# Six up units of every chunk in seven block products, gate and up units in another order, weight sums on semaphores of their own

## The reference, cut to what matters

```python
h = rms_norm(x, norm_ffn[layer])                       # 256 x 2048
x = x + (silu(h @ w_gate) * (h @ w_up)) @ w_down       # 2048 x 5632, 2048 x 5632, 5632 x 2048
```

## Time and profile before

| what | us |
|---|---|
| median of 3 runs | 1379.51 |
| lowest and highest of them | 1379.26, 1391.07 |
| the profiled execution, its own time | 1378.64 |
| its span, first to last instruction | 1376.9 |
| PE busy in the span | 1362.5 (99%) |
| DVE busy | 922.5 (67%) |
| ACT busy | 702.5 (51%) |

### The profile page before, as it was taken

The page is one execution under the profiler, slowest core; times in us unless marked ns, Lnnn a source line. Parts: engine busy times, 40 slices in busy tenths (PEclk is TensorE's granted clock), DMA queues, the critical chain, the costliest instruction groups (busy, mean ns, idle before and its releaser), DMA issues.

```text
span 1376.9 us, 26434 instructions
## 1 busy us (share of the span) xinstructions
PE 1362.5 (99%) x11280; PEld 1325.5 (96%) x11280; DVE 922.5 (67%) x1192; ACT 702.5 (51%) x913; POOL 44.9 (3%) x70
## 2 busy tenths in 40 slices
PE   8999999999999999999999999999999999999997
PEld 7888999999999999999999999999999999999997
DVE  5554557667655657666787888875446778887554
ACT  6343356656545655465645554544334455545444
POOL 3000010000000110000000000000000000000111
PEclk9999999999999999999999999999999999999999
DMA  7776655444565666546556655565555565666653
GB/s 241 246 231 219 186 171 156 140 152 146 154 192 168 194 203 218 184 168 201 165 182 194 217 181 181 182 214 208 191 198 184 184 214 169 193 196 231 210 198 123
DMA packets 135264, 261.08 MB, mean 190 GB/s; under 512 B 8448, under 2 KB 25408, under 8 KB 134768
## 3 DMA queue, kind: packets, MB, share of 16 engines
q1 hardware_dynamic: 132912, 251.13, 57.0%
q0 software_dynamic: 1792, 7.57, 1.6%
q10 hardware_dynamic: 448, 0.76, 0.2%
HBM read 257.33 MB, written 2.10 MB: 188 GB/s over the span
## 4 chain that ended last, share of the span: by engine, by line
PE 88%; DVE 7%; ACT 2%; DMA 2%; issue 1%; ACTq 0%; DVEq 0%
PE bank L646 24%; PE bank L647 23%; PE bank L648 23%; PE bank L885 4%; PE bank L887 4%; PE bank L888 4%; DVE weight_lo_ring L1322 2%; PE bank L634 2%; DVE weight_sums_lo L1342 1%; ACT weight_hi_ring L1071 1%; DMA raw_ring<-in_w_up 1%; DVE weight_sums L1331 1%; PE bank L784 1%; DVE act_rows L1382 1%; PE bank L695 1%
## 5 line engine op out<-in xcount | busy, mean ns | idle before, releaser
L1322 DVE TENSOR_TENSOR weight_lo_ring<-raw_ring,weight_hi_ring 128x1024 fp32r<-128x1024 f32 (+2 forms) x479 | 579.9, 1221 | 319.2 <-ACT weight_hi_ring L1071 263.9
L1071 ACT ACTIVATE weight_hi_ring<-raw_ring 128x1024 fp32r<-128x1024 f32 (+2 forms) x431 | 446.2, 1047 | 343.4 <-PE bank L648 271.0
L646 PE MATMUL bank<-weight_hi_ring,hT_hi 128*128 128x256 f32 (+2 forms) x1276 | 380.9, 298 | 0.0
L648 PE MATMUL bank<-weight_hi_ring,hT_lo 128*128 128x256 f32 (+2 forms) x1276 | 375.5, 294 | 0.0
L647 PE MATMUL bank<-weight_lo_ring,hT_hi 128*128 128x256 f32 (+2 forms) x1276 | 375.5, 294 | 0.0
L646 PEld LDWEIGHTS bank<-weight_hi_ring,hT_hi 128*128 128x128 f32 x1276 | 239.8, 188 | 10.0 <-issue 3.4
L647 PEld LDWEIGHTS bank<-weight_lo_ring,hT_hi 128*128 128x128 f32 x1276 | 239.9, 188 | 6.1
L648 PEld LDWEIGHTS bank<-weight_hi_ring,hT_lo 128*128 128x128 f32 x1276 | 239.6, 188 | 6.3
L646 PE MATMUL bank<-weight_hi_ring,h2T_hi 128*128 128x256 f32 x704 | 196.5, 279 | 3.2 <-DVE weight_lo_ring L1322 3.1
L648 PE MATMUL bank<-weight_hi_ring,h2T_lo 128*128 128x256 f32 x704 | 195.3, 277 | 0.0
L647 PE MATMUL bank<-weight_lo_ring,h2T_hi 128*128 128x256 f32 x704 | 195.3, 277 | 0.0
(11 more groups left out here) (253 smaller groups left out, 1897.0 us busy)
## 6 DMA issues: line engine op xcount, KB each, us to landing
raw_ring<-in_w_in SPq DMA_DIRECT2D x96, 512.0 KB, 3.4
raw_ring<-in_w_gate SPq DMA_DIRECT2D x88, 512.0 KB, 4.3
raw_ring<-in_w_up SPq DMA_DIRECT2D x88, 512.0 KB, 4.2
raw_ring<-in_w_down SPq DMA_DIRECT2D x88, 512.0 KB, 3.9
raw_ring<-in_w_in SPq DMA_DIRECT2D x55, 480.0 KB, 4.2
raw_ring<-in_w_out SPq DMA_DIRECT2D x32, 512.0 KB, 4.0
raw_ring<-in_w_br_c SPq DMA_DIRECT2D x16, 256.0 KB, 3.9
raw_ring<-in_w_br_a SPq DMA_DIRECT2D x16, 256.0 KB, 6.8
```

The source lines that it names most:

```text
L646: pe.matmul(dst, x_hi, w_hi, start=opening, stop=False, skip_group_check=True)
L648: m = pe.matmul(dst, x_lo, w_hi, start=False, stop=last and k == UK - 1, skip_group_check=True)
L1071: act.activation(whi[:, s, :, 0:width(u)], raw[:, s, :, 0:width(u)], ACT.Copy)\
L1322: dve.tensor_tensor(lo, w, hi.bitcast(F32), ALU.subtract).then_inc(lo_ready, 1)
```

## The change

`SEVEN` takes unit 7 too, so 66 instead of 55 up units are done in seven products. Unit 7 is the last of its chunk, so the last product of each bank may now stand in a unit of seven (`stop`). The order of units in the middle of a half becomes u4 of the chunk before, g0, g1, g2, its u5, its u6, its u7, g3, g4, u0, g5, g6, u1, g7, u2, u3. ACT writes a unit's own hi first and its weight sums' hi after it; DVE writes the unit's own lo, then the sums' lo; the sums have two semaphores of their own, and PE waits for the second in the middle of the unit, after four of the seven products. `lo_of_act` on DVE comes three units later than before, except in the last chunk of a half.

```diff
-SEVEN = (0, 1, 2, 4, 5)
+SEVEN = (0, 1, 2, 4, 5, 7)
...
-            plan += g[0:6] if i == a else [g[0], last[4], g[1], last[5], g[2], last[6], last[7], g[3], g[4], g[5]]
-            plan += [up[0], g[6], up[1], g[7], up[2], up[3]]
+            plan += g[0:5] if i == a else [last[4], g[0], g[1], g[2], last[5], last[6], last[7], g[3], g[4]]
+            plan += [up[0], g[5], g[6], up[1], g[7], up[2], up[3]]
...
+ACT_LO_AT = {v if i + 1 in (b for _, b in HALVES) else v + LAG: i for v, i in ACT_T_AT.items()}
...
                 into(i, 6, 0, block(0, 0), quarters(u, 0, 0), True)
-                into(i, 3, 0, block(1, 0), quarters(u, 1, 0), False)
-                into(i, 2, 0, total(3), quarters(u, 1, 1), False)
+                into(i, 3, 0, block(1, 0), quarters(u, 1, 0), stop)
+                into(i, 2, 0, total(3), quarters(u, 1, 1), stop)
                 into(i, 6, 1, total(1), quarters(u, 0, 1), True)
+                pe.wait_ge(ext_ready, N_SEVEN[u] + 1)
                 into(i, 7, 0, total(0), extra(0), True)
                 into(i, 7, 1, total(2), extra(1), True)
-                return into(i, 2, 1, block(1, 1), extra(2), False)
+                return into(i, 2, 1, block(1, 1), extra(2), stop)
...
                 if is_seven(u):
-                    n = N_SEVEN[u]
-                    act.wait_ge(w_summed, n + 1)
-                    if n >= 2:
-                        act.wait_ge(unit_used, SEVENS[n - 2] + 1)
-                    act.activation(ext_hi[:, n % 2, :, :], t_sum[:, :, :], ACT.Copy)
+                    act.wait_ge(w_summed, N_SEVEN[u] + 1)
                 else:
                     act.wait_ge(raw_ready[s], landed(u))
                 act.activation(whi[:, s, :, 0:width(u)], raw[:, s, :, 0:width(u)], ACT.Copy)\
                    .then_inc(hi_ready, 2 if u == 1 else 1)
+                if is_seven(u):
+                    n = N_SEVEN[u]
+                    if n >= 2:
+                        act.wait_ge(unit_used, SEVENS[n - 2] + 1)
+                    act.activation(ext_hi[:, n % 2, :, :], t_sum[:, :, :], ACT.Copy).then_inc(ext_hi_ready, 1)
...
                 if n >= 1:
-                    dve.wait_ge(lo_ready, SEVENS[n - 1] + 1)
+                    dve.wait_ge(ext_ready, n)
...
+                split_unit(u % RING, u + 1, width(u))
                 if is_seven(u):
-                    e = N_SEVEN[u] % 2
-                    dve.wait_ge(hi_ready, u + 1)
-                    dve.tensor_tensor(ext_lo[:, e, :, :], t_sum[:, :, :], ext_hi[:, e, :, :].bitcast(F32), ALU.subtract)
-                split_unit(u % RING, u + 1, width(u))
+                    n = N_SEVEN[u]
+                    dve.wait_ge(ext_hi_ready, n + 1)
+                    dve.tensor_tensor(ext_lo[:, n % 2, :, :], t_sum[:, :, :], ext_hi[:, n % 2, :, :].bitcast(F32),
+                                      ALU.subtract).then_inc(ext_ready, 1)
...
-                if v in ACT_T_AT:
-                    lo_of_act(ACT_T_AT[v])
+                if v in ACT_LO_AT:
+                    lo_of_act(ACT_LO_AT[v])
```

More of the change, by code:

```diff
@@ L419, in build_layer @@
         w_summed = sem("weights_summed")
+        ext_hi_ready = sem("weight_sums_hi_ready")
+        ext_ready = sem("weight_sums_ready")
         silu_ready = sem("silu_ready")
```

## The result

The changed kernel took 1363.82 us (median of 4 executions, 1363.79 to 1364.32); the kernel before 1380.35 (median of 4, 1379.26 to 1391.07: the three shown above and one more, 1381.19). The ratio is 0.9864, 95% interval [0.9815, 0.9913]: 1.4% faster. The profiled execution took 1363.83 with a span of 1362.1, which is 14.8 us less than in the earlier trace rows. The walk had made it 1364.1.

What follows compares the result with a forecast made beforehand. PE was taken as the bound, sometimes waiting for DVE. Gains of 3.7 (matmuls), 6.5 (waits) and 4.4 (wide spacing), 14.6 in all, took 1378.64 to 1364.1; 0.9 for the median gave 1365.0 us, range 1362.8 to 1371.8.

Steps and rivals of the forecast that it cites:

- The walk: Step-by-step timing of one chunk in the new order, used for the waits; the summed forecast for the profiled execution was 1364.1.
- Term 1: Unit 7 of 11 chunks loses 3 matmuls each on PE: 33 x 0.1133 = 3.7 us gained.
- Term 2: Added sums work per chunk, 2.7 us on DVE and 0.76 on ACT, hidden: DVE 39.9 against PE 42.36 us.
- Term 3: PE's waits for DVE in the feed-forward chunks go, except 0.7 us in the first chunk: 6.5 of 7.2 gained.
- The margins of a middle chunk: Time by which DVE's results precede PE's need in the new order; least 1.45 us, at g5.
- Term 4: Wider matmul spacing on PE, 4.4 ns more per matmul, goes with the waits: 4.4 us gained.
- rival (a): First-chunk margin missed, wide spacing for two or three chunks plus 1 us of waits: 1370; chance 0.22.
- rival (c): Wide spacing starts in the first chunk and never breaks off in gate, up and down units: 1392; chance 0.05.
- The step to the median: Added 0.9 us, the earlier runs' median above their profiled execution, taking 1364.1 to 1365.0.
- the line of 1%: Threshold for faster by over 1%, 13.8 us, falling at 1365.7; chance of beating it 0.50.
- Rival (b): Waits stay, moved to g5 or u0, as DVE has lost its margin; only matmuls go: 1375.8; chance 0.09.
- Rival (d): New mid-unit wait stops PE's weight loads running ahead, 66 times some 0.1, 6.6 us: 1371.6; chance 0.09.

Runs made afterwards that it cites:

- the fourth experiment: Changed kernel with unit 7 back to eight products; 1366.13 us, ratio 0.9934 to the kernel before.
- e6: Changed kernel with the old unit order and the old place of the activations' lo; 1366.36 us, ratio 0.9917 to the kernel before.
- e5: Changed kernel with the old order of work inside a unit and the old semaphore; 1380.22 us, ratio 1.0017 to the kernel before.
- e10: Changed kernel with the lo of the activations on DVE back behind u1, not u4; 1363.28 us, ratio 0.988 to the kernel before.
- e1: Kernel before with unit 7 done in seven products and nothing else; 1389.7 us, ratio 1.0107 to the kernel before.
- the second experiment: Kernel before with only the order inside a seven-product unit and its semaphores changed, old unit order, five units; 1366.31 us, ratio 0.9933.

## Why the prediction was right or wrong

**Term 1, 3.7 us: right.** The clean span moves by 4 us with unit 7. From the first gate unit on, the fourth experiment takes 717.7 us and the one with the early table 713.9; neither has a wait. The difference is 3.8.

**Term 2: right for the changed kernel, by a reason of which I had only half.** 28 us more on DVE were hidden there. But the sum of DVE's work against PE's chunk is not what decides. Unit 7 alone would have fitted by that sum and cost 16 us of waits, since DVE's lo also sets when SP loads. The prediction named the loads in one sentence and priced them at nothing. Both of my wrong expectations on parts of the change (unit 7 alone, the order alone) fail at this step, and the one on unit 6 fails because a sum of busy times has no place for a round trip that nothing fills.

**Term 3: right in size, 6.5 against 7.2 - 0.2 = 7.0.** The margins of a middle chunk are right to 0.3 us and were tested from both sides. In the first chunk I kept 0.7 and it was 0.2, at the place where the margin was least. Which edit does it: the inner order alone removes every wait; the unit order alone leaves as much waiting as there was. I had credited both. What the order is worth beside unit 7 is not settled: without it (e6) one execution has 2.1 us of waits and much wide spacing, and two others are as fast as the changed kernel.

**Term 4, 4.4 us: 3.5.** The spacing came in once more, in the first chunk, for ten units, as in rival (a) but for shorter and without its 1 us of waits. "With the waits gone I expect it gone" is right where they are gone: three profiles without waits have none of it. The error was to take it as gone with 0.1 us of waiting left. One reading was wrong as well: under rival (c) a wide stretch was said to have outlived two sets of transposes. That stretch (673 to 754 us) outlived those at 709 and ended behind the next; a second one (862 to 894) outlived one set too.

**Not in the sum:** 0.55 us, by which the feed-forward stage began earlier (647.00 for 647.55). So 14.6 forecast against 14.8 between the profiles is in part luck: term 3 was 0.5 too small, term 4 0.9 too large, and 0.55 came from elsewhere.

**The step to the median: this is the step that failed.** The prediction went from 1364.1 to 1365.0 because the median of the kernel before stood 0.9 us above its profiled execution, as if that distance belonged to the changed kernel too. The runs show the contrary: the changed kernel's median and its profiled execution are 0.01 us apart (1363.82 and 1363.83), and its four executions lie within 0.6 us (on the second chip 0.5 apart, within 2.8). The distance is the scatter of the kernel before, whose 51 other executions in this study lie between 1374.2 and 1390.5, and with the fourth run of the first chip it was 1.7 us and not 0.9. So a gain of 14.8 us between the profiles is 16.5 between the medians, where the prediction had 14.5. Its 1365.0 is 0.9895 of the 1379.51 that it started from, the fast end of its range, 1362.8, is 0.988, and the measured ratio is 0.9864. The range took in what could happen to the changed kernel; it had no term for which executions of the kernel before it is divided by, though their spread, 1379.26 to 1391.07, was on the table. That the line of 1% "falls right beside my forecast" was blind to the same thing. Why the kernel before scatters so is argued in the last section and not shown: one execution of it was profiled.

**Rival (b)** (DVE has lost its margin, waits moved to g5 or u0) is false here; waits at u0 are what the kernels without the inner order show (8.1 us in e5). **Rival (d)** is false: in mid-unit PE did not wait in any chunk, and a clean chunk is 42.37.

## What to carry to other kernels

Where an engine both makes an operand and frees a slot of a ring, its lateness is paid twice, once to the consumer and once through the load that it holds back; walk the ring, not only the sum of busy times. In such a queue do first what others wait for, and what is needed later after it: two copies in the other order and a semaphore for each were worth more (8.8 us between medians) than the arithmetic saved (3.7), and made the saving possible. Where a result comes back from another engine, see that other work stands ready for that time: with unit 6 in seven products there was none, and 1.19 us were lost in each of two units a chunk. Forecast a ratio with the scatter of both kernels in it. And give the first pass of a loop its own look: table loads and second norms sit there.

## What the runs showed of the hardware

The same stream of matmuls of 256 columns runs at one of two spacings, 0.1133 and 0.1177 us, at a granted clock of 1.00 and with PE fully busy. In the fourteen profiles every lasting switch stands at the start of a unit whose first or second matmul comes late (0.128 us or more behind the one before it), mostly after a wait or after transposes, and a spacing holds for 3 to some 220 us (in e6, from 883 to 1104). Restarts that look the same are not: behind the same wait of 0.1 us at g0 of the second chunk, the changed kernel went on wide in both its profiles and e10 went on narrow. Of restarts out of the narrow spacing, not behind transposes, all 16 whose second matmul came 225 or 226 ns behind the first went on wide, 9 of the 11 with 192 or 193 ns, and 9 of the 80 with 220 to 224 ns: a pattern, but not a rule. Behind transposes 7 of 127 did, all of them in e1 with a wait of PE behind the transposes.

So a short wait costs its own length and, by chance, 1.6 us a chunk behind it (369 x 0.0044), and that would explain why the kernel before, with many waits, scatters from 1374 to 1391, and the second experiment, with none, only from 1366.0 to 1366.8. What picks the spacing stays open; no run here tried to set it.
